# Mixer projection: one 512-column stream for both parts of the operand, with the halves of the bank added by VectorE

## The reference, cut to what matters

```
proj = h @ mix_w_in
xp, q, k, v, z, b_raw, a_raw, g_pool, g_dn = jnp.split(proj, MIX_IN_SPLITS, axis=-1)
...
qkv = jax.nn.silu(causal_depthwise_conv(jnp.concatenate([q, k, v], axis=-1), conv_w))
...
o = rms_norm(o, dn_norm_g)... * jax.nn.silu(z)
merged = jax.nn.sigmoid(g_pool) * ya + jax.nn.sigmoid(g_dn) * yb
```

## Time and profile before

| | before |
|---|---|
| median of 3 runs | 3097.82 us (3093.21 to 3102.21) |
| the profiled execution | 3102.03 us, its span 3100.4 us |
| mean granted TensorE clock | 0.957 |
| PE / DVE / ACT / POOL busy | 2892.7 / 2273.0 / 1368.8 / 178.9 us |
| the projection's 52 units | about 246 to 400 us of the span |

### The profile page before, as it was taken

One profiled execution on the slowest core, in us unless ns is written; L12 is line 12 of the kernel. 1 busy time (PEld: TensorE's weight loads), 2 busy tenths in 40 slices (PEclk: granted clock), 3 DMA queues, 4 the chain that ended last, 5 costly groups with the idle time before them and its releaser, 6 DMA issues.

```text
span 3100.4 us, 61090 instructions
## 1 busy us (share of the span) xinstructions
PE 2892.7 (93%) x22296; PEld 2683.1 (87%) x22296; DVE 2273.0 (73%) x3757; ACT 1368.8 (44%) x1977; POOL 178.9 (6%) x190
## 2 busy tenths in 40 slices
PE   5999988889989789999999999998899999999998
PEld 4998966779989789989998878898899999988787
DVE  6778634476778677988889976645569878799765
ACT  3445522244444445554434445544445544344454
POOL 0111003110111010020000000000000200000000
PEclk8999977899999989999999999999899999999999
DMA  8884520076867565544445445453345444454454
GB/s 311 304 290 147 189 70 1 17 248 231 305 230 279 194 234 183 178 160 156 162 149 170 163 169 191 163 164 121 124 151 180 162 156 160 146 169 167 163 192 139
DMA packets 150159, 549.52 MB, mean 177 GB/s; under 512 B 16672, under 2 KB 16928, under 8 KB 149664
## 3 DMA queue, kind: packets, MB, share of 16 engines
q1 hardware_dynamic: 127008, 463.00, 43.9%
q0 software_dynamic: 22320, 81.80, 7.6%
q10 hardware_dynamic: 720, 3.17, 0.3%
HBM read 546.86 MB, written 1.05 MB: 177 GB/s over the span
## 4 chain that ended last, share of the span: by engine, by line
PE 68%; DVE 10%; ACT 2%; issue 1%; POOLq 0%; DVEq 0%; POOL 0%; ACTq 0%
PE acc L1932 15%; PE st L1523 11%; PE st L1527 11%; PE st L1524 10%; PE acc L1938 7%; DVE w_lo L770 3%; PE st L1903 3%; PE acc L1523 2%; PE acc L1524 2%; PE acc L1527 2%; DVE arena L1216 1%; ACT w_hi L406 1%; PE acc L1863 1%; PE st L1570 1%; DVE arena L1212 1%
## 5 line engine op out<-in xcount | busy, mean ns | idle before, releaser
L770 DVE TENSOR_TENSOR w_lo<-ring,w_hi 128x1024 fp32r<-128x1024 f32 x864 | 1075.0, 1245 | 534.4 <-ACT w_hi L406 526.8
L406 ACT ACTIVATE w_hi<-ring 128x1024 fp32r<-128x1024 f32 x864 | 910.9, 1055 | 938.3 <-PE st L1527 772.5
L1523 PE MATMUL st<-h_hi,w_hi 128*128 128x256 f32 x3952 | 985.4, 287 | 6.8 <-ACT arena L698 3.5
L1524 PE MATMUL st<-h_lo,w_hi 128*128 128x256 f32 x3952 | 973.2, 284 | 0.0
L1523 PEld LDWEIGHTS st<-h_hi,w_hi 128*128 128x128 f32 x3952 | 760.5, 192 | 18.8 <-issue 10.2
L1524 PEld LDWEIGHTS st<-h_lo,w_hi 128*128 128x128 f32 x3952 | 761.3, 193 | 0.0
L1527 PE MATMUL st<-h_hi,w_lo 128*128 128x256 f32 x3952 | 558.8, 284 | 10.6 <-DVE w_lo L770 10.5
L1527 PEld LDWEIGHTS st<-h_hi,w_lo 128*128 128x128 f32 x3952 | 512.0, 193 | 14.6 <-DVE w_lo L770 14.4
L1932 PE MATMUL acc<-w_hi,act_hi 128*128 128x512 f32 x1016 | 322.7, 399 | 3.9 <-DVE act_lo L1336 3.9
L1932 PE MATMUL acc<-w_hi,act_lo 128*128 128x512 f32 x1016 | 316.0, 392 | 0.0
L731 ACT ACTIVATE act_hi<-arena 128x256 fp32r (+1 forms) x256 | 106.6, 418 | 409.0 <-PE acc L1938 400.8
(11 more groups left out here) (284 smaller groups left out, 3021.4 us busy)
## 6 DMA issues: line engine op xcount, KB each, us to landing
ring<-weights SPq DMA_DIRECT2D x864, 512.0 KB, 3.3
arena<-ada_weights POOLq DMA_DIRECT2D x152, 512.0 KB, 5.1
arena<-ada_weights SPq DMA_DIRECT2D x16, 512.0 KB, 13.2
arena<-const ACTq DMA_DIRECT2D x1, 2112.0 KB, 8.2
x_t<-params SPq DMA_DIRECT2D x1, 1024.0 KB, 11.3
extra<-crows POOLq DMA_DIRECT2D x2, 512.0 KB, 3.7
out<-arena POOLq DMA_DIRECT2D x1, 1024.0 KB, 4.2
extra<-crows SPq DMA_DIRECT2D x1, 512.0 KB, 3.8
```

Of the source, the lines that this page charges most:

```text
L406: nc_a.activation(w_hi[:, u % 2, :], ring[:, u % RING, :], ACT.Copy).then_inc(hi_ready, 1)
L770: v.tensor_tensor(w_lo[:, u % 2, :], ring[:, u % RING, :], w_hi[:, u % 2, :], ALU.subtract)\
L1523: mm(dst(t), w, hi_t(t), start=start, stop=False, skip_group_check=True)
L1524: mm(dst(t), w, lo_t(t), start=False, stop=False, skip_group_check=True)
```

## The change

What changes in the operand's buffers: `h_hi` and `h_lo` become the two halves of one tensor, `h_both`, so that for each slice of 128 rows the high and low parts stand side by side, 512 columns. For units 2 to 51 of the projection TensorE issues, per slice, one matmul of 512 columns with `w_hi`, which puts w_hi x h_hi into the left half of the bank and w_hi x h_lo into the right half. The 8 matmuls with `w_lo` go to the left half as before. Each unit now has a bank for itself, and ScalarE copies only the left half to SBUF (a plain copy for all units); VectorE then adds the right half to it in place (`right_half`). SiLU and sigmoid of the gates become instructions of their own on the sum in SBUF, one pair later. Units 0 and 1 are computed as before, each in a bank of its own.

```diff
-        h_hi = sb("h_hi", [P, DT, T], F32R)
-        h_lo = sb("h_lo", [P, DT, T], F32R)
+        h_both = sb("h_both", [P, DT, 2, T], F32R)
+        h_hi, h_lo = h_both[:, :, 0, :], h_both[:, :, 1, :]
...
+        def proj_dst(u):
+
+            if u < 4:
+                return xp[:, u, PADP:PADP + T]
+            if u < 28:
+                return qkv_raw[:, u - 4, 3:3 + T]
+            return (z_s, g_pool, g_dn)[(u - 28) // 8][:, (u - 28) % 8, :]
...
-            for p in range(14):
-                steps(U_MIX + 2 * p, 2)
...
-                nc_a.activation(dst, src, ACT.Copy).then_inc(sem("proj_out"), 1)
-                if p >= 4:
...
-            for p in range(14, 26):
...
-                nc_a.activation(dst, src, ACT.Silu if m < 4 else ACT.Sigmoid).then_inc(sem("proj_out"), 1)
+            def conv_silu(m):
+
+                eng.wait_ge(sem("conv"), m + 1)
+                nc_a.activation(qkv[:, 2 * m:2 * m + 2, :], qkv[:, 2 * m:2 * m + 2, :], ACT.Silu).then_inc(sem("qkv_silu"), 1)
+
+            def gate_of(p):
+
+                m = p - 14
+                dst = (z_s, g_pool, g_dn)[m // 4][:, 2 * (m % 4):2 * (m % 4) + 2, :]
+                eng.wait_ge(sem("proj_out"), 2 * p + 2)
+                nc_a.activation(dst, dst, ACT.Silu if m < 4 else ACT.Sigmoid).then_inc(sem("gate_done"), 1)
+
+            for u in range(N_MIX):
+                p = u // 2
+                steps(U_MIX + u, 1)
+
+                nc_a.activation(proj_dst(u), st[:, u % 4, 0:T], ACT.Copy).then_inc(sem("proj_half" if u > 1 else "proj_out"), 1)
+                if u % 2 == 1:
+                    if 4 <= p < 16:
+                        conv_silu(p - 4)
+                    if p > 14:
+                        gate_of(p - 1)
+            gate_of(N_MIX // 2 - 1)
...
-                eng.wait_ge(sem("proj_out"), m + 3)
+                eng.wait_ge(sem("proj_out"), 2 * m + 6)
...
+            def right_half(u):
+
+                eng.wait_ge(sem("proj_half"), u - 1)
+                v.tensor_tensor(proj_dst(u), proj_dst(u), st[:, u % 4, T:2 * T], ALU.add).then_inc(sem("proj_out"), 1)
+
             for p in range(26):
-                steps(U_MIX + 2 * p, 2)
+                for u in (2 * p, 2 * p + 1):
+                    step(U_MIX + u)
+                    if u > 1:
+                        right_half(u)
                 if 3 <= p < 15:
                     conv(p - 3)
...
-            eng.wait_ge(sem("proj_out"), 2)
+            eng.wait_ge(sem("proj_out"), 4)
...
-            pairs(U_MIX, 26, "proj_out", 0, 1)
+            def wide(u, bank):
+
+
+                eng.wait_ge(hi_ready, nth(u))
+                for t in range(DT):
+                    mm(st[:, bank, :], w_hi[:, u % 2, t * P:(t + 1) * P], h_both[:, t, :, :], start=t == 0, stop=False,
+                       skip_group_check=True)
+                eng.wait_ge(taken, u + 1)
+                for t in range(DT):
+                    ins = mm(st[:, bank, 0:T], w_lo[:, u % 2, t * P:(t + 1) * P], h_hi[:, t, :], start=False,
+                             stop=t == DT - 1, skip_group_check=True)
+                ins.then_inc(used, 1)
+
+            first_two(U_MIX, [st[:, 0, 0:T], st[:, 1, 0:T]], 1, False)
+            for u in range(2, N_MIX):
+                if u >= 4:
+                    eng.wait_ge(sem("proj_out"), u - 3)
+                wide(U_MIX + u, u % 4)
```

More of the change, by code:

```diff
@@ L501, in _ @@
             norm(1, shift1(1), U_MIX + 1)
-            for p in range(14):
-                steps(U_MIX + 2 * p, 2)
[L504 to L508, removed]
-                nc_a.activation(dst, src, ACT.Copy).then_inc(sem("proj_out"), 1)
-                if p >= 4:
[L512 to L515, removed]
-            for p in range(14, 26):
-                steps(U_MIX + 2 * p, 2)
[L518 to L522, removed]
+            def conv_silu(m):
+                eng.wait_ge(sem("conv"), m + 1)
+                nc_a.activation(qkv[:, 2 * m:2 * m + 2, :], qkv[:, 2 * m:2 * m + 2, :], ACT.Silu).then_inc(sem("qkv_silu"), 1)
+            def gate_of(p):
                 m = p - 14
                 dst = (z_s, g_pool, g_dn)[m // 4][:, 2 * (m % 4):2 * (m % 4) + 2, :]
-                src = st[:, p % 4, :].rearrange("p (u t) -> p u t", u=2)
-                nc_a.activation(dst, src, ACT.Silu if m < 4 else ACT.Sigmoid).then_inc(sem("proj_out"), 1)
+                eng.wait_ge(sem("proj_out"), 2 * p + 2)
[10 more added lines that the diff above has]
+            gate_of(N_MIX // 2 - 1)
             eng.wait_ge(sem("ba_psum"), 1)
```

## The result

The changed kernel takes 3107.17 us, median of 11 runs (3103.76 to 3109.38), against 3101.94 us for 11 runs of the kernel before: ratio 1.0022, 95% interval 1.0013 to 1.0031 (the quotient of the two medians alone is 1.0017). It is slightly slower, by less than the 0.3% that I had called no change. A second set of 11 runs gave 1.0016 (1.0007 to 1.0025). The prediction was 3101.7, range 3094 to 3109.

The account below looks back on a forecast made before the run. TensorE and VectorE were both taken as full in the convolution pairs, VectorE half idle behind them. +0.9 (start), +5.0 (convolution pairs) and -2.0 (tail) sum to +3.9 us on 3097.82: 3101.7 us, range 3094 to 3109.

Parts of the forecast that it names:

- no change: Whole kernel: a difference under 0.3% (9.3 us) can't be told from none; chance 0.86.
- The start: First convolution: GpSimd begins later, behind the add of unit 3, so its chain ends 0.9 us later; bounds +0.9, -2.
- The convolution pairs: Pairs 4 to 14: VectorE becomes the bound, 6.21 us a pair instead of 5.76, +5.0 us over 11 pairs.
- the forecast's "nothing" for the clock: After TensorE's first stall: a clock drop costs nothing; only staying at 1.2 GHz would cost +54 us, chance 0.02.
- a margin for the even unit: Convolution pairs after the first stall: TensorE may come up to 2.9 us late without holding VectorE.
- my signs of being wrong: Projection: a VectorE pair of 5.8 us or less, adds waiting for ScalarE's copy, or 1.2 GHz between 285 and 345 us.
- The tail: Units 33 to 51, behind the convolutions: TensorE's pace again, 0.107 us gained in each of 19 units, -2.0 us.
- The adds' wait for ScalarE: VectorE's adds in the projection: ScalarE's copy is done 0.9 us ahead of the add's turn, so no wait.
- The rule of the Trainium skill that I weighed: Wide matmuls: 2.5 ns issue floor, 1 us in 50 units; rival that they save nothing, total +5.5 us, chance 0.08.
- the row that I went by: Later stage's trace: matmuls of 512 columns take 0.2267 us each, against 0.240 for two of 256.
- the list of what would show it: Profile after: 6.2 us VectorE pairs, 11 TensorE stalls of 0.6 to 0.7 us, a first of 3 to 4 us.
- The point forecast for the whole: Whole kernel: 3101.7 us, from +3.9 us on the shown runs' median of 3097.82.

Follow-up runs that it names:

- the fastest variant: The changed kernel with the convolution's first multiplies on ScalarE and GpSimd's pooling started behind the convolutions: units 146.65 us, ratio 0.9978 to the kernel before, again 0.9979.
- its twin: The kernel before, without wide streams, with first multiplies on ScalarE and GpSimd's pooling behind the convolutions: units 151.04 us, ratio 0.9980, again 0.9976.

## Why the prediction was right, step by step

The forecast was +3.9 us for the projection, 3101.7 in all; the units lost 3.89 and 3.82 us. The mechanism stood: VectorE, with two adds more in a pair, became the bound of the convolution pairs at 6.21 us, and TensorE waited for it. Term by term, from the first profile (times from the projection's first matmul, at 245.89 before and 247.95 after):

- **The start, forecast +0.9, measured +0.29.** The first `w_lo` matmuls behind the first convolution came at 283.02 - 247.95 = 35.07 us, before at 280.67 - 245.89 = 34.78. The mechanism was right, the size was not. In the changed kernel's timelines of GpSimd, VectorE and TensorE:

```profile
264.59 7.09 POOL L1462 TENSOR_TENSOR arena<-arena 128x1024 f32<-128x1024 f32 x4 [19.94 <-DVE arena L961]
...
276.52 2.41 POOL L1470 TENSOR_TENSOR arena<-arena 128x1024 f32<-128x1024 f32 x1
...
276.10 2.98 DVE L950 TENSOR_SCALAR arena<-arena,par 128x256 f32<-128x256 f32 x2
276.51 2.57 DVE L950 TENSOR_SCALAR arena<-arena,par 128x256 f32<-128x256 f32 x1
...
283.02 2.08 PE L1657 MATMUL st<-h_both,w_lo 128*128 128x256 f32 x8 [2.73 <-DVE w_lo L776]
```

  GpSimd started 16.64 us after the first matmul instead of 15.53, 1.1 later; but its last instruction took 2.41 us and not 3.28, so the whole ended only 0.55 later (30.98 against 30.43), and part of that was still hidden. The two multiplies took 2.98 us and came out with the end of GpSimd's last instruction (279.08 and 278.93); the row at 276.51 is the second of them by itself, and it alone took 2.57. The Trainium skill ("SBUF — State Buffer", section "Who interferes with whom") has such an instruction locked out by GpSimd's; the row agrees, and so do the 5.03 us of six multiply-adds with two SBUF inputs. It also says that the one that starts first gets the port. This trace can't test that: the multiply that waited and GpSimd's instruction start within 0.01 us of each other (276.51, 276.52), and GpSimd's times in a profile are rough.
- **The convolution pairs, forecast 11 x 0.45 = 4.95, measured 5.15.** From 283.02 to the same matmuls of unit 32, at 351.63, are 68.61 us for 11 pairs; in the kernel before they were 344.13 - 280.67 = 63.46, by the row

```profile
344.13 1.12 PE L1527 MATMUL st<-h_hi,w_lo 128*128 128x256 f32 x8
```

  Ten of VectorE's pairs took 6.21 or 6.22, as forecast. One took 6.50, and that is where the forecast's "nothing" for the clock was off:

```profile
287.96 1.22 DVE L776 TENSOR_TENSOR w_lo<-ring,w_hi 128x1024 fp32r<-128x1024 f32 x1
...
289.71 1.22 DVE L776 TENSOR_TENSOR w_lo<-ring,w_hi 128x1024 fp32r<-128x1024 f32 x1 [0.20 <-ACT w_hi L414]
...
294.46 1.22 DVE L776 TENSOR_TENSOR w_lo<-ring,w_hi 128x1024 fp32r<-128x1024 f32 x1
```

  After the stall TensorE's granted clock was 0.59 in 283 to 287 us (the kernel's busy times by stretch),

```profile
283.00:287.00 4.00, 3.98 (x15) 3.55 (x16) 3.93 (x9) 1.33 (x2) 0.00 (x0) 0.59 0.63 179
```

  so it came late enough for `w_hi` of unit 13, by 0.2 us, that VectorE had to wait once. I had worked out a margin for the even unit only; the odd unit's is smaller. The rest of TensorE's loss was covered, as forecast. One of my signs of being wrong, a clock of 1.2 GHz between 285 and 345 us, came up for a little over 1 us (granted 0.50 from 285 to 286 us, 1.00 from 286.5 on); it cost these 0.3 us and did not last.
- **The tail, forecast -2.0, measured -1.55.** From unit 32 to the last unit 404.80 - 351.63 = 53.17 us, before 398.85 - 344.13 = 54.72. A unit takes 2.79 us and not 2.773: the wide matmul's spacing is 1.84 / 8 = 0.230 us (355.48 to 357.32), where the later stage of the earlier trace rows showed 0.2267. There two matmuls in a row have the same stationary operand and different banks, here each has another; which of these makes the 3 ns I have not tried.
- **The adds' wait for ScalarE: none**, as forecast. ScalarE's part of the changed kernel's timeline shows the copy for the pair above,

```profile
300.81 0.36 ACT L526 ACTIVATE arena<-st 128x256 f32<-128x256 f32 x1
```

  done at 301.17, 0.63 us ahead of the add at 301.80.

0.29 + 5.15 - 1.55 = 3.89. The terms' errors, -0.6, +0.2 and +0.45, cancel: that the sum comes out this near is luck, that VectorE's pair does is not. The rule of the Trainium skill that I weighed ("TensorE: Matmul & The Clock Gate", section on the back-to-back issue gap) would have the wide stream save 2.5 ns for each pair of matmuls; here it saves 0.240 - 0.230 = 10 ns, between the rule and the row that I went by, and nearer to the row.

In the list of what would show it, the stalls in front of the `w_lo` matmuls of even units were there, but nine of them, from 301.94 on, and not eleven: TensorE, late from its slow clock, had no gaps in the first two pairs. The first stall was 2.73 us, not 3 to 4. They read 0.36 in the brackets where I had written 0.6 to 0.7; by distance of rows they are 0.62.

The point forecast for the whole was 5.5 us low, mostly because it started from a median of three runs, 3097.82, where 11 to 35 runs give 3102. The medians show 5.2 and 4.5 us. The interval of the second ratio, 2.2 to 7.8 us, holds the units' 3.9; that of the first, 4.0 to 9.6 us, begins just above it, and in its profile the rest is the start of the projection, 2.06 us later, which the other runs show to be scatter (245.89 to 248.43 over all of them).

## What to carry to other kernels

Where two engines are both full in one stage, work moved from one to the other turns a gain into a loss even if each instruction looks cheap: compare the free-running pace of each engine, read where it is late and waits for nothing, not its share of the span. Where one engine is the bound only for a stretch, look for a part of its work there that an idle engine can do: ScalarE took two of eight instructions, and the gain of the streams landed inside the projection, though the medians of the whole kernel do not show it.

## What the runs showed of the hardware that I had not expected

**A short stall can cost more than itself.** Stalls of 1.8 to 1.9 us left TensorE's clock at 2.4 GHz; stalls of 2.04, 2.36 and 2.73 us at the same place were each followed by a stretch at 1.2 GHz (granted 0.66, 0.66 and 0.59 over the windows given above). Where TensorE set the pace this cost 1.5 us more, nearly as much as the stall; where VectorE did, 0.3. The length of the stall alone does not decide it: after 2.24 us in the kernel without adds the clock stayed up,

```profile
280.33 1.22 PE L1655 MATMUL st<-h_both,w_lo 128*128 128x256 f32 x8 [2.24 <-DVE w_lo L776]
283.23 1.12 PE L1655 MATMUL st<-h_both,w_lo 128*128 128x256 f32 x8
```

and its mean over 278 to 288 us was 1.00.

**What lies behind can differ by 4 us in one kernel.** The stage from the pooling's first matmul to the first one of the second feed-forward holds the same instructions in all kernels. Busy times of that stretch in the kernel before and in the fastest variant's first profile:

```profile
414.90:686.00 271.10, 225.88 (x1408) 191.66 (x1408) 139.48 (x222) 72.29 (x125) 43.28 (x29) 0.81 0.21 73
```

```profile
409.17:676.27 267.10, 222.02 (x1408) 188.87 (x1409) 139.45 (x222) 72.45 (x125) 43.26 (x29) 0.83 0.21 74
```

The same work, 271.1 us at a mean clock of 0.81 and 267.1 at 0.83. The fastest variant had 267.10 in its first profile and 271.21 in its second, its twin 267.39 and 270.0, the kernel with the adds twice 267.13, the changed kernel 271.63 and 271.6. TensorE is idle for 45 us of this stretch in either, and the clock was lower by 0.02 in the longer one; that the clock's steps fall differently is my reading of it, which no run isolates. That is as large as the effect under study: it gave back 4 us of what the adds twice lost. For the twins the profiles do not show it: the stages differ by 0.3 us in their first profiles and by 1.2 in their second, and the profiled spans lie 7.2 and 4.1 us apart in favour of the wide streams (3088.2 and 3095.4, 3095.0 and 3099.1), so what levels their medians is in runs that were not profiled. Whether the place at which the projection ends decides this, or chance alone, the profiles don't settle; it stays open.
